# Modulation rows taken first in their job on VectorE, in a two-layer hybrid encoder with a mixture of experts

## The reference

```
mod = silu(c) @ ada_w[l] + ada_b[l]           # 6 * 1024 values: sh1, sc1, g1, sh2, sc2, g2
h = rmsnorm(x) * (1 + sc1) + sh1
proj = h @ w_in[l]                            # inputs of four token mixers A..D, and the gates
branch = [y_A, y_B, y_C, y_D] @ w_branch[l]   # attention of four kinds, each projected
x = x + g1 * (sum(sigmoid(gate) * branch) @ w_out[l])
h = rmsnorm(x) * (1 + sc2) + sh2
x = x + g2 * (shared_expert(h) + routed_experts(h))   # 64 experts, top 6
```

## Time and profile before

| | |
|---|---|
| median of 3 runs | 3112.56 us (3110.33 to 3114.7) |
| the profiled execution's own time | 3112.57 us |
| its span in the profile | 3110.9 us |
| TensorE busy | 2867.5 us, 92% of the span |
| VectorE busy | 2032.6 us, 65% |
| ScalarE busy | 1584.7 us, 51% |
| mean granted TensorE clock | 0.968 of full speed |

### The profile page before, as it was taken

One profiled execution on the slowest core, in us unless ns is written; L12 is line 12 of the kernel. 1 busy time (PEld: TensorE's weight loads), 2 busy tenths in 40 slices (PEclk: granted clock), 3 DMA queues, 4 the chain that ended last, 5 costly groups with the idle time before them and its releaser, 6 DMA issues. The chain is left out here.

```text
span 3110.9 us, 42263 instructions
## 1 busy us (share of the span) xinstructions
PE 2867.5 (92%) x13740; PEld 2177.8 (70%) x13740; DVE 2032.6 (65%) x2885; ACT 1584.7 (51%) x2482; POOL 648.4 (21%) x563
## 2 busy tenths in 40 slices
PE   5999998899899999999779999989997999999994
PEld 4677776677677777777556777756775777777774
DVE  4544445565588888888835444465545888888886
ACT  2342423442357777777533334244323677777772
POOL 1000000000034553333110000000001456433330
PEclk9999999999899999999889999999998999999997
DMA  7123342233569999999612243313334899999985
GB/s 227 63 88 139 104 135 89 71 123 130 204 223 362 356 366 368 359 368 357 265 63 73 96 134 114 135 62 101 115 122 175 332 358 355 361 373 361 361 325 220
DMA packets 124556, 671.47 MB, mean 216 GB/s; under 512 B 27628, under 2 KB 29036, under 8 KB 90444
## 3 DMA queue, kind: packets, MB, share of 16 engines
q1 hardware_dynamic: 91040, 605.91, 52.4%
q0 software_dynamic: 31424, 57.44, 5.5%
q10 hardware_dynamic: 1932, 6.16, 0.9%
HBM read 656.60 MB, written 55.28 MB: 229 GB/s over the span
## 5 line engine op out<-in xcount | busy, mean ns | idle before, releaser
L2135 DVE TENSOR_TENSOR ew_lo<-ew,e_hi 128x2048 fp32r<-128x2048 f32 x258 | 591.9, 2294 | 184.1 <-ACT e_hi L1934 181.7
L707 PE MATMUL bank<-h_hi,w_hi 128*128 128x512 f32 x1248 | 516.4, 414 | 57.7 <-DVE w_lo L641 24.4
L1934 ACT ACTIVATE e_hi<-ew 128x2048 fp32r<-128x2048 f32 x260 | 497.4, 1914 | 79.1 <-PE bank L2341 79.1
L641 DVE TENSOR_TENSOR w_lo<-raw,w_hi 128x1024 fp32r<-128x1024 f32 x198 | 242.5, 1225 | 426.4 <-ACT w_hi L633 425.8
L707 PE MATMUL bank<-h_hi,w_lo 128*128 128x512 f32 x1248 | 505.7, 405 | 0.0
L707 PE MATMUL bank<-h_lo,w_hi 128*128 128x512 f32 x1248 | 504.1, 404 | 0.0
L2341 PE MATMUL bank<-e_hi,x_hi 128*128 128x512 f32 x1040 | 418.2, 402 | 0.1
L2341 PE MATMUL bank<-ew_lo,x_hi 128*128 128x512 f32 x1040 | 407.5, 392 | 0.0
L2341 PE MATMUL bank<-e_hi,x_lo 128*128 128x512 f32 x1040 | 405.4, 390 | 0.0
L633 ACT ACTIVATE w_hi<-raw 128x1024 fp32r<-128x1024 f32 x198 | 208.3, 1052 | 278.9 <-DMA raw<-in_wmix 161.9
L707 PEld LDWEIGHTS bank<-h_hi,w_hi 128*128 128x128 f32 x1248 | 241.7, 194 | 145.4 <-issue 53.1
(11 more groups left out here) (317 smaller groups left out, 4400.6 us busy)
## 6 DMA issues: line engine op xcount, KB each, us to landing
ew<-in_wexp SPq DMA_DIRECT2D x130, 2048.0 KB
raw<-in_wmix SPq DMA_DIRECT2D x297, 512.0 KB, 4.0
ew<-in_wexp SPq DMA_DIRECT2D x130, 1024.0 KB
ew<-y_d SPq DMA_DIRECT2D x8, 2048.0 KB, 14.5
ew<-y_d SPq DMA_DIRECT2D x8, 1024.0 KB, 7.7
ada0a<-in_ada SPq DMA_DIRECT2D x2, 2048.0 KB, 13.5
ada0b<-in_ada SPq DMA_DIRECT2D x2, 2048.0 KB, 22.2
h_d<-htok ACTq DMA_DIRECT2D x8, 512.0 KB, 12.7
```

The lines of the kernel that those rows point to most:

```text
L641: nc.vector.tensor_tensor(w_lo[q % SPLIT][:], raw[u % RAW][:], w_hi[q % SPLIT][:].bitcast(F32), ALU.subtract).then_inc(lo_done, 1)
L707: ins = nc.tensor.matmul(out, lhs, rhs, start=start, stop=stop)
L1934: nc.scalar.activation(e_hi[h][:], up_part(ew, j, h), ACT.Copy).then_inc(whi_done, 1)
L2135: nc.vector.tensor_tensor(up_part(ew_lo, j, h), up_part(ew, j, h), e_hi[h][:].bitcast(F32), ALU.subtract).then_inc(wlo_done, 1)
```

## The change

In `events_of`, the modulation events of a job are emitted when the walk is at the job's first product and before its `tile` event, instead of behind its `chunk` event at the last product. On VectorE the order in a job with a modulation tile goes from

`split_lo(next weight tile)`, `dve_out(job)`, `ada(tile)` to `ada(tile)`, `split_lo(next weight tile)`, `dve_out(job)`.

ScalarE ignores `ada` events. The stream of tiles, the order of the loads and the number of instructions are the same. In an attention stage, where a job spans several steps, the `ada` event also goes to the step in which the job starts.

```diff
                 todo = products(j)
                 for i in range(i0, i1):
                     u = todo[i][0]
+                    if i == 0:
+                        ev += [("ada", v) for v in j.after]
                     if u is not None and (i == 0 or todo[i - 1][0] != u) and all_jobs_first[u] == (j.c, i):
                         ev.append(("tile", u))
                     if i == len(todo) - 1:
                         ev.append(("chunk", j.c))
-                        ev += [("ada", u) for u in j.after]
             return ev
```

## The result

| | before | after |
|---|---|---|
| median of 4 runs each, us | 3111.44 (3107.56 to 3114.70) | 3055.26 (3054.47 to 3058.53) |
| ratio, with its 95% interval | | 0.9818 (0.9805 to 0.9831) |
| profiled execution's span, us | 3110.9 | 3056.9 |
| its mean granted TensorE clock | 0.968 | 0.969 |
| six stretches gbA, gbB, gbD of both layers, us | 510.6 | 458.5 |

The change saves 56.2 us by the medians.

The account below looks back on a forecast made before the run. TensorE was taken to bound the mixer block, with 37.1 us idle in gbA, gbB and gbD. Sum: 3112.57 - 34.6 (waits) + 1.6 (tile 81) - 10.0 (slow clock) = 3069.6 us; range 3060 to 3094.

Parts of the forecast that it names:

- The ring: In gbA, gbB and gbD: late load, late split, late modulation row, late load three tiles on; 17.0 us of `w_lo` waits.
- the branch results' waits: In gbA, gbB and gbD: TensorE's 12 waits for branch results to be taken out, 17.6 us, all go.
- The attention stages: Moved rows mostly vanish in VectorE's idle time there; bounds -2 to +8.0 us, taken 0.
- The signs: Afterwards SyncE's wait for rows about half of 987.9 us, ScalarE's under 40, TensorE's for `w_lo` about 12, idle below 5.
- that of the clock: Rival: the 50 long matmuls come somewhere else in the mixer block; 3079.6 us, chance 0.27.
- only the waits on `w_lo` had gone: Rival: branch results stay behind the split on VectorE, so TensorE still waits for the bank; 3095.6 us, chance 0.11.
- had the ring stayed: Rival: VectorE reaches the row only after the last event, so nothing gets earlier; 3112.6 us, chance 0.06.
- had the rows pushed the splits back: Rival: each moved row puts 1.21 us on VectorE ahead of `w_lo`; slower, 3120.6 us, chance 0.06.
- the term of the sum for the waits: In gbA, gbB and gbD: 34.6 us of TensorE's waits go, 1.6 us stays.
- tile 81: In gbB: the one tile per layer still late; 0.8 us of its 3.33 us wait stays, twice, 1.6 us.
- The 10.0 us: In gbA, gbB and gbD: 50 slow-clock matmuls behind waits, 0.20 us each, go with the waits; bounds 0 to 10.0.
- the six runs that I had counted: In gbA, gbB and gbD: stretches of 8, 7, 7, 8, 7 and 13 slow matmuls, each behind a wait.

Follow-up runs that it names:

- gb_only: Rows first only in the gate and branch jobs of gbA, gbB and gbD, otherwise the kernel before: 3066.99 us, ratio 0.9838.
- att_only: Rows first only in the attention stages, last in gbA, gbB and gbD, otherwise the kernel before: 3115.78 us, ratio 1.0007.
- double_rows: The changed kernel with one more VectorE pass of 1.2 us over the tile ahead of each row: 3067.90 us, ratio 0.9854 to the kernel before.
- the change again: The changed kernel timed a second time, unchanged, beside the kernel before: 3066.68 us, ratio 0.9863.
- thin_rows: The kernel before, order kept, with a layer's 48 rows handed out otherwise so that gbA, gbB and gbD carry 4 each: 3139.79 us, ratio 1.0088.

## Why the prediction missed, though its mechanism held

**What held.** The ring: a row queued behind a late split holds the buffer that the third next load wants. The stall lies in the gb stretches alone (gb_only, att_only), ends when the row goes first, and the branch results' waits were a consequence of it. The attention stages, priced between -2 and +8 us and taken at 0, gave nothing that can be measured (ratio 1.0007, the interval 5.6 us to either side). The signs held: SyncE's wait for rows about half (495.9 of 987.9), ScalarE's for transfers under 40 (18.4), TensorE's for `w_lo` about 12 (10.5), idle time in the windows under 5 us (4.5), granted clock 1.00. The rivals are out; that of the clock is told below. If only the waits on `w_lo` had gone, those of L792 would be there; had the ring stayed, nothing would be; had the rows pushed the splits back, double_rows would have shown it at twice the price.

**What failed: the term of the sum for the waits, 34.6 - 1.6 = 33.0 us.** It was mis-sized, and the stretches show by how much. I added up what the rows give in brackets as idle time. But a row's idle time runs from the modelled end of the last matmul, 0.39 us long, while the next would have started 0.23 us behind it. Timeline of TensorE before, around the wait of 1.66 us in the earlier trace rows (the matmul that waited started at 296.93, between these two):

```profile
294.87 0.39 PE L707 MATMUL bank<-h_hi,w_lo 128*128 128x512 f32 x1
...
297.23 0.40 PE L707 MATMUL bank<-h_lo,w_hi 128*128 128x512 f32 x1
```

From start to start it is 296.93 - 294.87 = 2.06 us, so 2.06 - 0.23 = 1.83 us were lost and not 1.66; and the next start comes 0.30 us later instead of 0.23. Counted in this way, as the excess of every start-to-start step over 0.227 us in the six stretches:

| us lost | before | after | gained | in my sum |
|---|---|---|---|---|
| at waits | 43.3 | 5.7 | 37.6 | 33.0 |
| slow-clock steps (61 and 8 of them) | 12.1 | 1.6 | 10.5 | 10.0 |
| all other steps | 39.5 | 35.6 | 3.9 | 0 |
| together | 94.9 | 42.9 | 52.0 | 43.0 |

In the third line 29.0 us of either kernel are no loss: they are other matmuls and transposes of the attention stage, which run between the mark and the first job. Of the 4.6 us at waits, some 0.9 is tile 81, for which I left 0.8 us in each layer; one of the two after the change:

```profile
468.63 0.47 PE L707 MATMUL bank<-h_hi,w_hi 128*128 128x512 f32 x1 [0.26 <-DVE w_lo L641]
```

The other is 0.48. The remaining 3.7 us are the model of a matmul's end, and of the 3.9 of the third line 3.2 are the first step after each wait, which took 0.30 to 0.34 us (0.56 to 0.59 in four cases where the clock was already low), and which I had at nothing. With the right sizes the sum would have been 3112.6 - 52.0 = 3060.6 us, just inside the range; the rest of the miss is 1.1 us by which the median before lies under the 3112.57 that I started from, and some 4 us outside the stretches.

**The clock.** The 10.0 us came out right in size, but the tie of slow steps to waits is looser than I had it. Of the 61 slow steps before, 47 stand in the six runs that I had counted (with three of the first steps of 0.56 to 0.59 they are my 50), and behind waits that the change takes away. None of them is left, and 47 x 0.2 = 9.4 us. The other 14 stand behind the wait before the first out job, one per layer, which the rows put down to `issue` and not to the ring, and which is as long after the change. TensorE at that wait, before (layer 1) and after (layers 1 and 2):

```profile
763.74 0.77 PE L707 MATMUL bank<-h_hi,w_hi 128*128 128x512 f32 x1 [2.16 <-issue]
764.30 0.63 PE L707 MATMUL bank<-h_lo,w_hi 128*128 128x512 f32 x1
...
739.14 0.47 PE L707 MATMUL bank<-h_hi,w_hi 128*128 128x512 f32 x1 [2.15 <-issue]
739.45 0.40 PE L707 MATMUL bank<-h_lo,w_hi 128*128 128x512 f32 x1
...
2240.31 0.55 PE L707 MATMUL bank<-h_hi,w_hi 128*128 128x512 f32 x1 [2.15 <-issue]
2240.66 0.63 PE L707 MATMUL bank<-h_lo,w_hi 128*128 128x512 f32 x1
```

Behind the same two waits there were 14 slow steps before, 8 after and none in the change again. So the other 1.1 us of the 10.5 are luck. The rule of the Trainium skill that I weighed against the 10.0 us ("TensorE: Matmul & The Clock Gate", "What's actually happening") says that a count of slow matmuls varies from run to run and shouldn't be fitted. The 14, 8 and 0 agree with it. Leaving the 10.0 us out, which gave 3079.6, was still the wrong use of it: in both traces of the changed kernel the slow steps behind the ring's waits went with the waits.

**The range** ended at 3060, and the prediction gives no reason for that end. Its terms already held all waits and all slow matmuls, and I took that for the most there was to gain. It wasn't, since idle time in the rows leaves out what a wait costs beside itself. And little room was left below for the scatter of stages that the change doesn't touch, though the three runs of the kernel before had themselves spread over 3110.3 to 3114.7. Of the 56.2 us of the first timing 52 are shown, in the trace, to be the change's; 4 are not explained, and the second timing doesn't have them.

## What to carry to other kernels

Where a few buffers are shared by loads issued in order, find the instruction that releases each and ask what stands ahead of it in its engine's list; if that waits for a later load, there is a ring, and its lap is to be compared with the bottleneck's work per lap. Put the release ahead of everything that waits, and don't add up the gains of the parts: half of the move gave three quarters of the gain, and a lighter load in one stage sent the ring into the next (thin_rows). And price a wait on TensorE from one matmul's start to the next one's, with the slower steps behind it: here the idle time in the rows was some 8 us of 52 too little.

## What the runs showed beside it

- The first step after a wait was 0.30 to 0.34 us instead of 0.23 while the granted clock was 1.00 (296.93 to 297.23 above, in a wait of 1.66 us); with the four of 0.56 to 0.59 at the low clock these steps came to 3.8 us over the six stretches before, and to 0.6 after.
- All eight waits of 1.8 to 3.9 us in the six stretches before had slow matmuls (0.43 us a step, granted clock 0.50) behind them, and no shorter one had; but of four waits of 2.15 us in the two traces of the changed kernel only one had.
- The same kernel against the same kernel before gave 0.9818 in one timing and 0.9863 in another, with its changed stretches alike to 1.7 us. For a change of this size, lengths between marks in the trace settle more than the ratio does.
